# A hybrid attention block: two neighbouring mixes of the memory attention become one of 512 columns, and a mix of the chunked attention moves up a quarter

## The reference, cut to what matters

```
hn   = rmsnorm(h, g_norm[l])
proj = hn @ w_in[l]
aq, ak, av, ag, bq, bk, bv, bg, mq, mg = split(proj)
a_out = swa_sink_attention(aq, ak, av, sinks, slopes)     # 8 heads, band of two 64-row chunks
b_out = rmsnorm(diff_attention(bq, bk, bv, lam), subln_g) # 4 heads, chunk-causal
# memory attention, 4 heads of 128, 256 memory rows
logits = einsum('bshd,bmhd->bhsm', mq, mk) * d ** -0.5
p      = softmax(logits)
m_out  = einsum('bhsm,bmhd->bshd', p, mv)
gated  = concat([a_out * silu(ag), b_out * silu(bg), m_out * silu(mg)])
y      = rmsnorm(h + gated @ w_out[l], g_final)
```

## Time and profile before

| | us |
| --- | --- |
| median of three runs (701.49 to 701.77) | 701.75 |
| the profiled execution, its own time | 701.2 |
| its span, first to last instruction | 699.4 |
| PE busy | 690.3 (99%) |
| DVE busy | 416.3 (60%) |
| ACT busy | 313.8 (45%) |
| POOL busy | 231.6 (33%) |
| granted TensorE clock, mean over the span | 0.999 |
| four heads on PE, start to start of the same place | 124.1 each |

### The profile page before, as it was taken

One profiled execution on the slowest core, in us unless ns is written; L12 is line 12 of the kernel. 1 busy time (PEld: TensorE's weight loads), 2 busy tenths in 40 slices (PEclk: granted clock), 3 DMA queues, 4 the chain that ended last, 5 costly groups with the idle time before them and its releaser, 6 DMA issues.

```text
span 699.4 us, 11598 instructions
## 1 busy us (share of the span) xinstructions
PE 690.3 (99%) x3933; PEld 579.2 (83%) x3933; DVE 416.3 (60%) x916; ACT 313.8 (45%) x733; POOL 231.6 (33%) x204
## 2 busy tenths in 40 slices
PE   8999999999999999999999999999999999999996
PEld 8888888888888888888888888888888888888885
DVE  6785245766754666675366677636666786533432
ACT  6763444456543444564344555433454654122200
POOL 5723132144323214333222434232333542322310
PEclk9999999999999999999999999999999999999999
DMA  9921211120052111005211110521140285514210
GB/s 298 311 62 32 60 33 30 31 61 2 1 153 60 31 31 42 20 1 151 61 31 31 31 31 1 149 62 31 31 124 1 66 259 166 163 61 135 80 58 35
DMA packets 79157, 52.73 MB, mean 75 GB/s; under 512 B 36080, under 2 KB 71936, under 8 KB 79104
## 3 DMA queue, kind: packets, MB, share of 16 engines
q1 hardware_dynamic: 79104, 52.06, 26.0%
HBM read 43.14 MB, written 8.91 MB: 74 GB/s over the span
## 4 chain that ended last, share of the span: by engine, by line
PE 95%; DVE 3%; DMA 1%; issue 0%; ACT 0%; SPq 0%; DVEq 0%; ACTq 0%
PE acc L1497 17%; PE acc L1498 17%; PE acc L1499 17%; PE score L1497 5%; PE score L1499 5%; PE score L1498 5%; PE trans L1499 3%; PE trans L1498 3%; PE trans L1497 3%; PE score L1702 3%; PE score L1704 2%; PE trans L1722 2%; PE mixo L1498 2%; PE mixo L1499 2%; PE mixo L1497 2%; PE score L1781 1%
## 5 line engine op out<-in xcount | busy, mean ns | idle before, releaser
L1497 PE MATMUL acc<-x_hi,w_hi 128*128 128x512 f32 x512 | 203.9, 398 | 0.2 <-DVE gates L1265 0.2
L1498 PE MATMUL acc<-x_lo,w_hi 128*128 128x512 f32 x512 | 200.2, 391 | 0.0
L1499 PE MATMUL acc<-x_hi,w_lo 128*128 128x512 f32 x512 | 200.0, 391 | 0.0
L942 POOL TENSOR_TENSOR w_lo<-w_raw,w_hi 128x512 fp32r<-128x512 f32 x66 | 85.2, 1312 | 184.9 <-ACT w_hi L610 166.8
L1499 PEld LDWEIGHTS acc<-x_hi,w_lo 128*128 128x128 f32 x512 | 96.2, 188 | 20.8
L1497 PEld LDWEIGHTS acc<-x_hi,w_hi 128*128 128x128 f32 x512 | 96.3, 188 | 19.3 <-issue 1.5
L1498 PEld LDWEIGHTS acc<-x_lo,w_hi 128*128 128x128 f32 x512 | 96.3, 188 | 16.8
L789 ACT ACTIVATE logits<-logits,stats_b 128x128 f32<-128x128 f32 (+7 forms) x64 | 49.3, 772 | 54.0 <-DVE stats_b L1294 54.0
L1286 DVE CUSTOM_DVE_ANT_0 logits<-score,b_bias 128x384 f32<-128x384 f32 (+5 forms) x96 | 49.8, 554 | 23.2 <-PE score L1704 23.0
L798 ACT ACTIVATE p_hi<-trans 128x512 fp32r<-128x512 f32 (+1 forms) x56 | 30.8, 566 | 62.9 <-PE trans L1722 41.7
L1313 DVE TENSOR_TENSOR p_lo<-trans,p_hi 128x512 fp32r<-128x512 f32 (+1 forms) x56 | 35.8, 651 | 33.1 <-ACT p_hi L798 33.1
(11 more groups left out here) (254 smaller groups left out, 1396.2 us busy)
## 6 DMA issues: line engine op xcount, KB each, us to landing
w_raw<-in_w_in SPq DMA_DIRECT2D x68, 256.0 KB, 3.4
mixed<-gates SPq DMA_DIRECT2D x9, 512.0 KB, 4.2
mix_raw<-mixed SPq DMA_DIRECT2D x8, 576.0 KB, 6.2
wo_raw<-in_w_out SPq DMA_DIRECT2D x8, 512.0 KB, 6.7
x_res<-in_x SPq DMA_DIRECT2D x8, 512.0 KB, 3.4
out_y<-y_row SPq DMA_DIRECT2D x16, 256.0 KB, 2.1
logits<-in_x SPq DMA_DIRECT2D x4, 512.0 KB, 7.9
wo_raw<-in_w_out SPq DMA_DIRECT2D x6, 256.0 KB, 5.8
```

The lines of the kernel that those rows point to most:

```text
L942: last = pool.tensor_tensor(w_lo[:, slot, cols], w_raw[:, slot, cols], w_hi[:, slot, cols].bitcast(F32), ALU.subtract)
L1497: pe.matmul(out, a_hi, b_hi, start=start, stop=False, skip_group_check=True)
L1498: pe.matmul(out, a_hi, b_lo, start=False, stop=False, skip_group_check=True)
L1499: return pe.matmul(out, a_lo, b_hi, start=False, stop=stop, skip_group_check=True)
```

## The change

The four mixes of the memory attention of a head, 256 columns each, become two pairs: `m_pair` reads both slots of `p_hi` and `p_lo` with one matmul of 512 columns and fills all of `mixo`, and one DVE operation of 512 columns gates it. The tables that number the mixes follow. In `BETWEEN`, mix 0 leaves quarter (6,1,2), mix 1 leaves (7,0,2), mix 2 leaves (7,0,3); pair 0 stands behind (7,0,1), pair 1 behind (7,1,0) where mix 3 was. `a_mix` 2 moves from (7,0,1) to (7,0,0). The data that is computed is the same.

```diff
-    (6, 1, 2): [("a_norm", 3), ("m_spread", 1), ("m_norm", 2), ("m_mix", 0)],
-    (7, 0, 0): [("m_scores", 3), ("b_fold", 1)],
-    (7, 0, 1): [("a_mix", 2), ("m_norm", 3), ("m_spread", 2)],
-    (7, 0, 2): [("m_mix", 1), ("b_low", 1)],
-    (7, 0, 3): [("m_spread", 3), ("m_mix", 2)],
-    (7, 1, 0): [("a_spread", 3), ("m_mix", 3), ("b_squares", 1)],
+    (6, 1, 2): [("a_norm", 3), ("m_spread", 1), ("m_norm", 2)],
+    (7, 0, 0): [("a_mix", 2), ("m_scores", 3), ("b_fold", 1)],
+    (7, 0, 1): [("m_norm", 3), ("m_pair", 0), ("m_spread", 2)],
+    (7, 0, 2): [("b_low", 1)],
+    (7, 0, 3): [("m_spread", 3)],
+    (7, 1, 0): [("a_spread", 3), ("m_pair", 1), ("b_squares", 1)],
...
+                def m_gate(pair):
+
+                    cols = slice(pair * HALF, (pair + 1) * HALF)
+                    dve.wait_ge(pt_done, at(PT_MIX[("m_spread", 2 * pair + 1)], h, NMIX))
+                    w = [n for n, _, _ in TILES].index("mg")
+                    dve.wait_ge(acc_free, at(2 * w + pair, h, 2 * NT, PRE_FREE))
+                    dve.scalar_tensor_tensor(out=gates["m"][:, cols], in0=mixo[:, :], scalar=0.5, in1=gates["m"][:, cols],
+                                             op0=ALU.mult, op1=ALU.mult).then_inc(o_free, 1)
...
-                def m_mix(m):
-                    out = o_bank(("m_mix", m))
-                    slot = p_slot(("m_spread", m))
+                def m_pair(pair):
+
+                    o_bank(("m_pair", pair))
+                    p_slot(("m_spread", 2 * pair + 1))
+                    out = mixo[:, :].rearrange("p (a n) -> p a n", a=2)
                     for j in range(2):
                         cols = slice(j * MEM, (j + 1) * MEM)
-                        last = product(out, mv_hi[:, j, :], mv_lo[:, j, :], p_hi[:, slot, cols],
-                                       p_lo[:, slot, cols], j == 0, j == 1)
+                        last = product(out, mv_hi[:, j, :], mv_lo[:, j, :], p_hi[:, :, cols], p_lo[:, :, cols],
+                                       j == 0, j == 1)
                     last.then_inc(pt_done, 1)
```

More of the change, by code:

```diff
@@ L174 @@
 PT_AT = numbered(*[s for s in HEAD if s[0] in ("b_spread", "m_spread")])
-PT_MIX = numbered(*[s for s in HEAD if s[0] in ("b_spread", "m_spread")])
-assert list(PT_MIX) == [(s[0][0] + "_spread",) + s[1:] for s in HEAD if s[0] in ("b_mix", "m_mix")]
+PT_MIX = numbered(*[("b_spread",) + s[1:] for s in HEAD if s[0] == "b_mix"])
+NMIX = len(PT_MIX) + 2
+PT_MIX.update({("m_spread", m): NMIX - 2 + m // 2 for m in range(4)})
+assert [s for s in HEAD if s[0] in ("b_mix", "m_pair")][-2:] == [("m_pair", 0), ("m_pair", 1)]
+assert [PT_AT[("m_spread", m)] % 2 for m in range(4)] == [0, 1, 0, 1]
 O_AT = numbered(*[s[:2] for s in HEAD
-                  if s[0] in ("m_mix", "a_mix") or (s[0] == "b_mix" and s[2] == s[1])])
+                  if s[0] in ("m_pair", "a_mix") or (s[0] == "b_mix" and s[2] == s[1])])
 NS, NTB, NPT, NO = len(S_AT), len(T_AT), len(PT_AT), len(O_AT)
@@ L182 @@
 assert NS % S_RING == 0 and NTB % T_RING == 0 and NPT % PT_RING == 0 and PRE_T % T_RING == 0
-NMIX = len(PT_MIX)
 def build(nc, x, mem, w_in, g_norm, a_sinks, lq1, lk1, lq2, lk2, subln_g, g_mem, w_mem_kv, w_out,
@@ L517, in spill @@
                 else:
-                    sp.wait_ge(o_free, at(O_AT[(f"{g}_mix", 3)], h, NO))
+                    sp.wait_ge(o_free, at(O_AT[("a_mix", 3) if g == "a" else ("m_pair", 1)], h, NO))
                 sp.dma_start(mixed_v[:, bass.ds(h * 3 + "abm".index(g), 1), :],
@@ L1314, in take_lo, with a_gate @@
                        .then_inc(t_free, 1)
-                def gate(g, m):
+                def a_gate(m):
                     cols = slice(m * MEM, (m + 1) * MEM)
[L1319 to L1323, removed]
+                    dve.wait_ge(a_mixed, at(m, h, 4))
+                    w = [n for n, _, _ in TILES].index("ag")
                     dve.wait_ge(acc_free, at(2 * w + m // 2, h, 2 * NT, PRE_FREE))
-                    dve.scalar_tensor_tensor(out=gates[g][:, cols], in0=mixo[:, 0:MEM], scalar=0.5,
-                                             in1=gates[g][:, cols], op0=ALU.mult, op1=ALU.mult)\
+                    dve.scalar_tensor_tensor(out=gates["a"][:, cols], in0=mixo[:, 0:MEM], scalar=0.5,
+                                             in1=gates["a"][:, cols], op0=ALU.mult, op1=ALU.mult)\
                        .then_inc(o_free, 1)
+                def m_gate(pair):
[5 more added lines that the diff above has]
+                                             op0=ALU.mult, op1=ALU.mult).then_inc(o_free, 1)
                 def b_take(g):
@@ L1433, in head @@
                             b_take(s[1])
-                    elif s[0] in ("m_mix", "a_mix"):
-                        gate(s[0][0], s[1])
+                    elif s[0] == "a_mix":
+                        a_gate(s[1])
+                    elif s[0] == "m_pair":
+                        m_gate(s[1])
                     elif s[0] == "m_scores":
@@ L1827, in head @@
                         m_spread(s[1])
-                    elif s[0] == "m_mix":
-                        m_mix(s[1])
+                    elif s[0] == "m_pair":
+                        m_pair(s[1])
                     elif s[0] == "a_scores":
```

## The result

| | before | changed |
| --- | --- | --- |
| median of six runs each | 701.69 (701.00 to 701.91) | 704.49 (704.29 to 705.25) |
| profiled execution, its own time | 701.2 | 704.56 |
| its span | 699.4 | 702.7 |
| granted TensorE clock | 0.999 | 1.000 |

The ratio is 1.0043, 95% interval 1.0032 to 1.0053: 2.8 slower, where 2.2 was forecast. The time lies 0.1 above the range.

A forecast was written before the change was run, and what follows sets the result against it. PE's matmul list and its waits on DVE's tail were taken to bound the kernel; -0.24 + 0.1 + 1.40 + 0.9 = +2.2 on a median of 701.75 gave 703.9, range 701.5 to 704.4.

The forecast's parts named there:

- Both meetings: Ends of first and second head: DVE's multiplication starts 0.03 and 0.05 behind POOL's second weight-tile piece and loses the port.
- the second wait: PE waits for the first bank, freed late behind DVE's jump, in two heads: 0.45 more each, 0.9 in all.
- what PE saves: PE's mixes as 512-column matmuls, less what the moved steps give back: 0.06 saved per head, 0.24 in four.
- the waits inside a head: PE's wait at pair 1 for its low part: 0 to 0.1 per head, taken as 0.03, 0.1 in all.
- What bounds the kernel: PE, busy 99% of the span: time moves by its list of matmuls and its waits on DVE's tail.
- The tail 0.26 later: The wide gate heads DVE's tail at each head's end; everything up to the multiplication comes 0.26 later against PE.
- The first waits: PE's waits behind the lost meetings of the first two heads: 0.71 and 0.69 with slow products, together 1.40.
- (1): Ends of the first two heads: DVE still wins both meetings, only PE's saving is left, 701.6; chance 0.20.
- (2): DVE loses, but idle time at the jump runs from the end of its work: +1.26, 703.0; chance 0.24.
- (3): DVE loses one meeting of the two: +0.6 to +1.0, 702.6; chance 0.06.
- (4): Faster by more than 0.2%, 1.4, which needs PE's saving six times as large; chance 0.02.
- (5): Waits at `m_spread` 3 and pair 1, held for hidden, are 0.2 each per head: +1.6, up to 705; chance 0.05.

The follow-up runs named there:

- the late tail: Kernel before with an added DVE copy of 176 columns ahead of the gate of each head's last memory mix: 704.01, ratio 1.0035.
- The kernel without the jump: Changed kernel with DVE's loop over the first three heads written out, so DVE never jumps back: 703.60, ratio 1.0029.
- the half gate: Changed kernel with the gate of pair 1 cut to its first 256 columns: 701.64, ratio 1.0001.
- the 48 columns: Kernel before with an added DVE copy of only 48 columns ahead of the gate of each head's last memory mix: 701.46, ratio 0.9997.

## Why the mechanism was right and the time came out above the range

The measured 704.49 lies above the range of 701.5 to 704.4. Both meetings were lost and both waits followed, as forecast; what failed are the sizes of two terms of the sum. The larger is the second wait ("and what is behind it"): it was put at 0.9 for both heads, with the time from the jump to the bias tables as in the kernel before, and measured 1.4. The other is what PE saves together with the waits inside a head: it was put at -0.24 + 0.1 and measured +0.2.

**What bounds the kernel: right.** PE's list of matmuls and its waits on DVE's tail account for 3.2 of the 3.3 between the profiled spans; the other 0.17 stands ahead of the first `b_squares` 0 and isn't explained.

**What PE saves: off by 0.1 per head.** Six matmuls of a pair take 1.37, 0.228 each, as forecast, and two slots in one operand cost nothing. But from `b_squares` 0 to 1 a head takes 0.03 to 0.08 more, where I had 0.06 less plus 0.03. About half of the miss is the wait for the low part ahead of pair 1. Timeline of the changed kernel:

```profile
182.32 0.68 DVE L1315 TENSOR_TENSOR p_lo<-trans,p_hi 128x512 fp32r<-128x512 f32 x1
...
182.72 0.60 PE L1803 MATMUL trans<-ident,a_probs 128*128 128x128 f32 x4
183.15 0.47 PE L1507 MATMUL mixo<-p_hi,mv_hi 128*128 128x512 f32 x1
183.46 0.39 PE L1508 MATMUL mixo<-p_lo,mv_hi 128*128 128x512 f32 x1
```

The transposes to the product take 0.43 instead of 0.35; with `b_squares` 1 in between they take 0.35 again. The low part ended when I said, 0.07 ahead of the due time, but it needed 0.15 from its end to PE's start, not 0.06: my release time came from another pair of operations. For the rest I summed the steps of head 0 by kind, changed minus before: the products of the mixes -0.26, those of the backbone +0.17, the scores, whose first now stands behind float32 matmuls, +0.11, the transposes of `m_spread` -0.06, those of `a_spread` with the wait +0.08. Without the wait PE saves 0.04 there, where I had 0.06. In heads 1 to 3 the backbone takes +0.20 or +0.21, and these further 0.03 I can't assign to a step. In sum the term was -0.1 and measured +0.2.

**The tail 0.26 later: right.** (The 0.8 for a multiplication that waits for nobody was misread, since alone it takes 0.69; the 0.55 by which it ended behind POOL's piece was read off a lost meeting, so the sum doesn't depend on it.) The shift against POOL was +0.26 and +0.28 (from -0.24 and -0.21 to +0.02 and +0.06), forecast starts +0.03 and +0.05 behind. That so small a distance decides was the weakest step of the prediction; it held.

**The first waits: right.** 0.63 and 0.60 over a normal step, 0.11 for the slow product behind each, forecast 0.62, 0.60 and 0.09.

**The second waits: mechanism right, too small.** Forecast 0.36 each, measured 0.57 and 0.63, and 0.1 of slow product behind each, so 1.4 instead of 0.9 for both. That DVE's idle time runs from the jump and not from the end of its work, which I had at 0.43 against 0.24, is shown by the waits list. Changed kernel, then the one with the late tail:

```profile
DVE b_bias L1222 <- issue: 3.6, 2, 1.9
```

```profile
DVE b_bias L1220 <- issue: 3.3, 2, 1.6
```

(us, count, mean.) It was 1.17. With the late tail `b_gate` took 0.45 less, since POOL was done, and the idle time grew by 0.48: the work behind the jump's start became shorter, the bias table came no earlier. From the jump, which the trace has as an instruction without busy time, to the first instruction behind it 2.8 to 3.1 passed in every one of these kernels with the loop. The size was off since it varies: 2.84 and 2.86 before, 3.00 and 3.09 in the changed kernel, 2.87 and 2.86 in the one with the late tail, whose second waits are 0.43 and 0.42, near the forecast. The added 0.16 and 0.23 of the changed kernel are most of the 0.21 and 0.27 by which its second waits exceed 0.36. Why this time varies stays open.

The Trainium skill, Runtime: NRT & Kernel Launch, section "Instruction fetch mechanics", explains such a gap by a fetch of the jump's target. The kernel without the jump agrees; that it is a fetch, no row shows. A jump alone doesn't cost this: in the changed kernel, behind the jumps of ACT, POOL and SP, whose loops are shorter (240 instructions and fewer, DVE's has 355), the next instruction comes after 0.24 to 0.31.

**Rivals.** (1), DVE still wins, is what the half gate and the 48 columns show one step earlier. (2) falls with the second waits, (3) with the two lost meetings, (4) with the time. (5) was right in place (pair 1), but 0.08 and not 0.2 per head. The term that put the time above the range is the second wait (+0.5), with the stretches of the mixes (+0.3); 2.2 + 0.8 = 3.0, and the sum of the stretches without the opening is 3.2.

## What to carry to other kernels

Where DVE and POOL come to a shared port within some tenths of each other, read both starts before you lengthen anything ahead of the one that PE waits for: starts that came 0.02 to 0.06 behind POOL's instead of 0.08 to 0.24 ahead cost 1.2 to 1.5 at the end of a head here, and the shorter products of the mixes saved 0.1 per head. Put an operation that is made wider behind the one on which the tail depends, not ahead of it. After a lost wait, ask what is queued behind it (here a jump, behind which 3 passed) before you count the loss once.

## What the runs showed of the hardware

The order of the starts decided all meetings of this multiplication: DVE went first at -0.33 to -0.04, POOL at 0.00 to +0.65, and the loser paid for the rest of the other's instruction (1.82 at +0.02, 1.48 at +0.37, for 0.69 alone). DVE went on 1.13 to 1.16 behind the start of a piece of POOL that the profile shows as 1.29 long. The Trainium skill, SBUF — State Buffer, section "SBUF: two separate sides", has the rule that whoever starts first keeps the port for its whole instruction; every row here agrees, and at a distance of 0.00 POOL had it.

A release from DVE to a product of PE took 0.06 after `evacuate` and 0.15 after the low part, so a cover of 0.1 should be counted as none.
